# Three changes of order: a triangle in mixer one, a routing table inside a product, and one weight load moved ahead

## What is computed

```python
def gated_delta_rule(q, k, v, g, beta):          # second half of mixer one, 4 heads of 128, chunks of 64
    decay = jnp.exp(jnp.where(causal, g[..., :, None] - g[..., None, :], -jnp.inf))
    kkt = jnp.einsum('bhncd,bhnsd->bhncs', k_beta, k) * decay
    a_mat = jnp.where(strict, kkt, 0.0) + jnp.eye(CHUNK, dtype=q.dtype)
    sol = lax.linalg.triangular_solve(a_mat, rhs, left_side=True, lower=True, unit_diagonal=True)
    qk = jnp.einsum('bhncd,bhnsd->bhncs', q, k) * decay

def hier_moe(h, ...):                            # 32 experts in 4 groups, two per token
    for each expert e:
        y = (jax.nn.silu(hf @ wg[e]) * (hf @ wu[e])) @ wd[e]
        acc = acc + gate[:, e:e + 1] * y
```

## Time and profile before

| | |
|---|---|
| time, median of 3 runs | 1407.87 us (1407.12 to 1408.49) |
| time of the profiled execution | 1413.08 us |
| its span, first to last instruction | 1411.3 us |
| mean granted TensorE clock | 0.984 |
| PE busy | 1326.8 us (94%) |
| DVE busy | 576.1 us (41%) |
| ACT busy | 333.1 us (24%) |
| POOL busy | 118.0 us (8%) |
| moved by DMA | 316.00 MB, mean 224 GB/s |

### The profile page before, as it was taken

The page is one execution under the profiler, slowest core; times in us unless marked ns, Lnnn a source line. Parts: engine busy times, 40 slices in busy tenths (PEclk is TensorE's granted clock), DMA queues, the critical chain, the costliest instruction groups (busy, mean ns, idle before and its releaser), DMA issues. The chain is left out here.

```text
span 1411.3 us, 19408 instructions
## 1 busy us (share of the span) xinstructions
PE 1326.8 (94%) x7876; PEld 630.4 (45%) x7876; DVE 576.1 (41%) x1236; ACT 333.1 (24%) x574; POOL 118.0 (8%) x276
## 2 busy tenths in 40 slices
PE   4999999999998995799999999999999999999997
PEld 2655536865455331233474444444444543333332
DVE  7749545445565331122658972000123542111006
ACT  5522432434111110010455551110001111111113
POOL 4100000001000110011300025000000000110000
PEclk9999999999999997899999999999999999999999
DMA  9811110155637799999741111312028288999994
GB/s 373 338 61 60 60 60 21 43 210 209 274 141 288 313 424 424 424 422 424 326 179 60 60 59 60 118 61 75 0 77 339 100 321 322 420 391 419 393 419 185
DMA packets 40938, 316.00 MB, mean 224 GB/s; under 512 B 6910, under 2 KB 6918, under 8 KB 20880
## 3 DMA queue, kind: packets, MB, share of 16 engines
q1 hardware_dynamic: 32808, 296.34, 52.5%
q0 software_dynamic: 7584, 17.33, 3.2%
q10 hardware_dynamic: 456, 1.08, 0.2%
HBM read 302.11 MB, written 22.56 MB: 230 GB/s over the span
## 5 line engine op out<-in xcount | busy, mean ns | idle before, releaser
L2811 PE MATMUL mix_ps<-y_t,store 128*128 128x512 f32 (+1 forms) x640 | 249.7, 550 | 1.4 <-ACT y_t L2892 1.4
L2811 PEld LDWEIGHTS mix_ps<-y_t,store 128*128 128x128 f32 x640 | 121.4, 190 | 127.2 <-issue 124.0
L2199 PE MATMUL m_ps<-store,par 128*32 128x512 f32 (+2 forms) x896 | 148.3, 594 | 0.0
L2199 PE MATMUL mix_ps<-store,par 128*32 128x512 f32 (+2 forms) x688 | 120.0, 618 | 26.3 <-DMA store<-in_gu 16.6
L1121 PE MATMUL mix_ps<-y_t,store 128*128 128x512 f32 x320 | 142.7, 599 | 0.0
L1121 PEld LDWEIGHTS mix_ps<-y_t,store 128*128 128x128 f32 x320 | 59.2, 190 | 71.6 <-issue 70.7
L2199 PEld LDWEIGHTS m_ps<-store,par 128*32 128x32 f32 (+2 forms) x896 | 46.1, 119 | 81.7 <-issue 81.7
L3129 DVE TENSOR_TENSOR store<-store,m_ps 128x512 f32<-128x512 f32 x8 | 5.5, 687 | 183.5 <-PE m_ps L3113 183.5
L2339 DVE TENSOR_TENSOR m2r_a<-m2r_a,m_ps 128x256 f32<-128x256 f32 x22 | 9.3, 421 | 170.7 <-ACT m2r_a L2260 170.7
L2199 PEld LDWEIGHTS mix_ps<-store,par 128*32 128x32 f32 (+2 forms) x688 | 36.5, 121 | 93.6 <-issue 93.6
L2221 PE MATMUL m_ps<-store,m2r_a 128*32 128x512 f32 (+2 forms) x448 | 76.3, 595 | 0.6 <-ACT m2r_a L2264 0.6
(11 more groups left out here) (735 smaller groups left out, 1848.3 us busy)
## 6 DMA issues: line engine op xcount, KB each, us to landing
store<-in_gu SPq DMA_DIRECT2D x54, 2048.0 KB, 16.1
store<-in_dn SPq DMA_DIRECT2D x54, 1024.0 KB, 17.1
store<-in_w_in SPq DMA_DIRECT2D x14, 2048.0 KB, 10.4
store<-in_w_ada SPq DMA_DIRECT2D x12, 2048.0 KB, 9.9
mods<-in_gu SPq DMA_DIRECT2D x10, 2048.0 KB, 13.8
mods<-in_dn SPq DMA_DIRECT2D x10, 1024.0 KB
store<-in_w_out SPq DMA_DIRECT2D x4, 2048.0 KB, 8.4
store<-y_rows SPq DMA_DIRECT2D x8, 1024.0 KB, 10.3
```

What stands on the lines that cost most here:

```text
L2199: last = pe.matmul(ps[who, 2 + j % 2, :], xt[:, k, who], w[:, k, :], start=(k == 0), stop=(k == KD - 1))
L2811: last = pe.matmul(pz[:, n % 4, cols], w[:, k, j * P:(j + 1) * P], m.a_t[:, k, cols], start=(k == 0), stop=(k == KD - 1))
```

## The change

It changes only orders. In mixer one, DVE builds tile 1's triangle directly behind tile 0's, before it bounds tile 2, and builds tile 2's before it bounds tile 3. In both expert stages PE runs the table after five of the eight k-steps of up(0) and the other three behind it, and DVE makes the token lists before times_up(0). In stage one SP issues unit 6's down part at j = 0, behind unit 6's gate and up part, and not at j = 1.

```diff
                 dve.wait_ge(lvc, 4)
-                bounded(0)
-                for t in range(NT):
-                    if t + 1 < NT:
+                for t in range(0, NT, 2):
+                    bounded(t)
+                    if t == 0:
+                        bounded(1)
+                    lower(t)
+                    if t:
                         bounded(t + 1)
-                    lower(t)
+                    lower(t + 1)
                 dve.wait_ge(x1, 4)
...
             for n in c.next_in(j):
                 load_up(sp, m, c, n, job_of(n))
-            for n in c.next_in(j - 1):
-                load_down(sp, m, c, n, job_of(n))
+            if j == 0 and HV == 1:
+                for n in c.next_in(0):
+                    load_down(sp, m, c, n, job_of(n))
+            if j > 1 or HV > 1:
+                for n in c.next_in(j - 1):
+                    load_down(sp, m, c, n, job_of(n))
...
-        def up(j):
+        def up(j, lo=0, hi=KD):
             i = j // HV
-            for n in dict.fromkeys(n for n, _ in c.steps[j]):
-                pe.wait_ge(c.gu_ready[c.slot(n)], 16 * c.uses(n))
-            for k in range(KD):
+            if lo == 0:
+                for n in dict.fromkeys(n for n, _ in c.steps[j]):
+                    pe.wait_ge(c.gu_ready[c.slot(n)], 16 * c.uses(n))
+            for k in range(lo, hi):
...
+        up(0, 0, 5)
+        x.table_products(pe)
+        up(0, 5)
         for j in range(NJ):
-            up(j)
             if j == 0:
-                x.table_products(pe)
                 turn_h(0)
                 if HV == 1:
                     down(0)
                     turn(1)
                 continue
+            up(j)
...
         for j in range(NJ):
-            times_up(j)
             if j == 0:
                 x.token_lists(dve)
+            times_up(j)
```

## The result

The changed kernel takes **1401.53 us** (median of 5 runs, 1399.61 to 1402.55) against 1408.49 us for the kernel before beside it (5 runs, 1407.12 to 1409.27). The ratio is 0.9944, with a 95% interval of 0.993 to 0.9959: 7.0 us faster. The forecast was 1396.3, in a range of 1394.0 to 1402.5; the time lies in the range, at the rival "gather no earlier", priced at 1401.4.

What follows compares the result with a forecast made beforehand. The first expert stage was taken as bound by bytes from 467 to 660 us, PE bounding the mixers and second expert stage. 3.75 + 4.85 + 2.45 + 0.5 = 11.55 us off the median gave 1396.3 us, range 1394.0 to 1402.5.

Steps and rivals of the forecast that it cites:

- gather no earlier: Stage one rival: the gather shares engines with unit 6's load and lands as before; saves 6.45 us, 1401.4 us; chance 0.15.
- Part 1: Mixer one: the triangle built earlier lets score(3) start without a gap at full clock; 3.75 us, bounds 2.3 and 3.75.
- the cover: Mixer one: x1 reaches 4 at 237.4, turn_x wants it at 239.4, leaving 2.0 us before delay costs time.
- Part 2: Stage one: the table inside up(0) starts the gather 2.6 us earlier, so the saturated stretch begins 4.85 us earlier.
- I take 7.1: Stage one: the gather of tile 1 assumed to take 7.1 us, near the earlier 6.8, so turn(1) starts at 452.4.
- The clock: Stage one: short idle pieces keep 2.4 GHz, so turn and copies take 1.87 us, not 2.75, and up(1) 7.0.
- Part 3: Stage one: unit 6's down part, issued when down(0) ends, moves into a DMA hole; 2.45 us less in the stretch.
- Stage two: Second expert stage: the earlier gather lands by 1150, so turn(1) starts at 1152.0 without waiting; 0.5 us.
- Slower: Rival: the gather is held up behind weights in both stages; at T = 16, 6.2 us slower, 1414.1; chance 0.03.
- not passed on: Stage one rival: loads hang on slots, or the down part displaces other traffic; saves 4.25 us, 1403.6; chance 0.10.
- queue dry: Rival: the queue runs dry at 471 us, losing the down part's 2.45; 1398.8 us; chance 0.17 shared with clock lost.
- T: The time a held-up gather takes; decides against the other gains from 12.9, slower by 0.2% needs 14.3.

Runs made afterwards that it cites:

- e11: The kernel before, with SP holding unit 6's gate and up load in stage one until the gather of tile 1 has landed: 1404.51 us, ratio 0.9958.
- e4: The changed kernel, with unit 6's gate and up load in stage one held until the gather of tile 1 has landed: 1398.65 us, ratio 0.9927.
- e10: The changed kernel with the table behind the whole of up(0) in stage one alone, and unit 6's gate and up load held: 1400.51 us, ratio 0.9927.
- e8: The changed kernel with unit 6's gate and up load held until the first gather lands, measured a second time: 1397.58 us, ratio 0.9902.
- e3: The changed kernel with unit 6's down part issued at j = 1 again, as in the kernel before: 1405.15 us, ratio 0.9965.
- e5: The changed kernel itself, measured again beside its variants on one chip: 1400.67 us, ratio 0.9936.
- e6: The changed kernel with unit 6's down part at j = 1 again, a second look at e3: one run, 1402.23 us.
- e9: The changed kernel with the table behind the whole of up(0) again in stage one alone, stage two keeping the new order: 1402.71 us, ratio 0.9958.
- e2: The changed kernel with the table behind the whole of up(0) and times_up ahead of the token lists in both expert stages: 1404.61 us, ratio 0.9957.
- e1: The changed kernel with the old order of bounded and lower in mixer one: 1406.86 us, ratio 0.9973.
- e12: The changed kernel with five more 512 column products between down(0) and the first turn in step 0: 1403.84 us, ratio 0.9956.

## Why the prediction came out as it did

The time fell into the range, but not by the mechanism that the forecast rested on: the largest term, 4.85 us, did not come, and the case that did, "gather no earlier", had a chance of 0.15. The saving was forecast at 11.55 us and measured at 7.0.

**Part 1: right.** Forecast 3.75, measured 3.78. lower(3) raised x1 at 234.71, 2.1 us before turn_x started behind product(19) at 236.80; the cover was forecast at 2.0. One remark: of the 3.75 only 2.3 are the gap. In e11 the gap is there (2.28) but score(3) ran at full clock, and product(19) came 7.87 us behind score(2), so in such an execution part 1 is worth 2.3. The forecast's lower bound was this.

**Part 2, stage one: the step that failed is "I take 7.1" for the gather's time.** The gather did start 2.57 us earlier against U, and up(0), times_up, turn_h and down(0) took their forecast places within 0.3 us (down(0) starts at U + 11.38; forecast 448.4 less 437.25, 11.15). But 7.1 was read from a gather that started when the load had been under way for 3.4 us, and carried to one with the whole load ahead of it. It took 9.2, 9.7, 9.7, 8.4 and 7.9 us in five profiles, and 4.6 in one. The sum of start and time hardly moved, so turn(1) came 0.2 us earlier, not 2.35. The rule of the Trainium skill that the prediction weighed ("DMA: Bandwidth & Descriptors", section "Queues, rings and completion order": an engine takes turns between queues, packet by packet) gave this rival. Its direction is borne out in stage one by e4, e10 and e11, where the gather without that load took 4.3 us or less, and by e8, where PE did not wait for it. It does not say how much is lost, and e3 and stage two show that the loss isn't certain: a gather that starts ahead of the load can get through in 4.2 to 5.1 us. The rival had a chance of 0.15; the median of all 25 gathers, 10.3, should have weighed more against the one at the same place.

**The clock: the second half of that term.** The forecast counted 2.5 us for a clock that stays full behind the turn, since the idle pieces were short. In the profile after there was an idle piece of 2.26 us and it fell; in e5 one of 2.76 and it did not, in e6 neither with 2.72, in before it did with 3.72. So this term, worth 2.3 us when it comes (28.99 less 26.69), is by execution. With the clock full (e5) part 2 and the clock together give 2.0 us at turn(2) against before's profile; with the fall, minus 0.3. Against e9 and e2, the old order with the clock's fall hidden in down(0), they give nothing: 26.12 and 26.34 there, 26.69 in e5.

**Part 3: right.** Forecast 2.45, measured 2.5 (76.6 to 77.4 against 79.2 to 80.0), and 2.2 between e5 and e6, which have the same turn(2). The stretch stayed fed, and its saving came on top of any of part 2, as said.

**Stage two: right in size.** Forecast 0.5, measured 0.58 (9.59 less 9.01 at its up(0)), no wait for the gather, turn_h open by 1.0 us. The forecast kept the gather's old time and only moved its start. In fact the gather also became faster: 7.2 to 7.5 us in the three profiles with the old order there (before, e2, e11), 4.2 to 5.1 in the eleven with the new one. The load goes out 1.6 us behind it, as in stage one, where five of the six such gathers whose landing is shown took 7.9 to 9.7. One difference is in the traces: in stage one the two parts of unit 5 go out at U + 1.3 and 2.5 and in stage two the two loads ahead at 0.3 and 0.6, so these land about 1 us earlier there (8.2 to 8.6 and 10.6 to 11.0 behind the start of up(0), in stage one 9.3 and 11.9 in e4). Whether that decides it was not tested. What the faster gather gave has no effect on the time, for turn(1) comes right behind up(1).

**Slower, not passed on, queue dry:** none of these. The gather held up "behind weights in both stages" held for one stage, and T was 9.7 at most, far from 12.9.

The sum with the measured terms: 3.78 + 0.2 + 2.5 + 0.6 = 7.1, less what the clock does, for 7.0 by the medians. The saving that was forecast can be had: with the load held stage one gives 7.36 us, where the forecast had 7.3, and the two ratios, 0.9902 and 0.9927, are 13.8 and 10.3 us, on either side of the forecast's 11.55. But e10 and e11 say that it isn't part 2 that brings it. It is the load that stands aside: 4.7 us on the kernel before by the medians beside each other (1409.21 and 1404.51), 3.1 on the changed one (1400.67 and 1397.58, e5 and e8). That the size is the forecast's is chance.

**A faster kernel**: the changed one with the held load, 0.9902 (0.9885 to 0.9918) and 0.9927 (0.9903 to 0.995), 10 to 14 us below before.

**What stays open**: why the gather got through in 4.6 us once in stage one with the load issued as always (e3) and did so each time in stage two, and what decides in which execution the clock falls at the turn. The median of 27 executions of before in one group, 1409.8 (1403.83 to 1414.77), spreads as widely as these terms would make it; that it is they was not shown. The 0.9 us behind the last expert step weren't looked into.

## What to carry to other kernels

A transfer's time depends on what is in flight beside it: before moving one earlier, list the loads that go out at the same time, and take its time from rows with the same company, as a range and not as one figure: the same order of issues gave 7.9 to 9.7 us at one place and 4.2 to 5.1 at another. Where a small transfer has a waiting engine behind it and a big one has 20 us of slack, try holding the big one back by one wait; here that was worth 4.7 us on the kernel before, against 7.0 for the three changes of order together, and 3.1 us on top of them. And read a stage from its own first instruction, because 2.65 us of the difference of the two spans arose ahead of every edit.

## What the runs showed of the hardware

- In stage one a gather of one tile took 3.1 to 4.3 us (e4, e10, e11) while unit 6's load was held and only the end of unit 5's was beside it, 6.6 to 6.8 when it started 3.4 us behind unit 6's load of 2 MB (before, e2, e9), and 7.9 to 9.7 (after, e1, e5, e6, e12), once 4.6 (e3), when that load was issued 1.5 us behind it.
- In stage two it took 7.2 to 7.5 us with the load 3.3 us ahead of it (before, e2, e11) and 4.2 to 5.1 with the load 1.6 us behind it (the other eleven). The gather of tile 2, which starts 1.5 us later, then took 9.4 to 10.7, and 6.7 to 7.1 in the old order.
- The load pays less: issued beside the gather of stage one it landed after 9.3 to 11.1 us, held until behind it after 7.9 to 8.8.
- The granted clock fell to 0.50 in down(0) in four of the five profiles with the old order in stage one, where PE had run the table's short matmuls ahead of it, and in none of the nine with the new order. The kernel before did not show that fall in its profile; there it came at the turn.
- Executions of kernels whose instructions up to there are the same reach score(2) at 222.96 us (e12) to 226.98 us (e10), before the first edited line acts on PE.
